# Decayed attention in two-level stages: products of 192 columns, a buffer of further decayed queries, and a seventh level of 64x64

## The reference, cut to what matters

```
S_t = diag(g_t) S_{t-1} + k_t v_t^T        o_t = S_t^T q_t
decay[i, j] = exp(sum of log g over j+1..i)     for j <= i
scores[i, j] = sum over d of  q[i, d] * k[j, d] * decay[i, j, d]
o[i] = sum over j <= i of scores[i, j] v[j]
```

## Time and profile before

| what | value |
|---|---|
| median of 3 runs | 1010.59 us (1009.25 to 1010.59) |
| the profiled execution's own time | 1010.97 us |
| its span, first to last instruction | 1009.1 us |
| PE busy | 989.7 us, 98% of the span |
| POOL busy | 752.5 us, 75% |
| DVE busy | 549.5 us, 54% |
| ACT busy | 486.5 us, 48% |
| mean granted TensorE clock | 0.990 |

### The profile page before, as it was taken

The page is one execution under the profiler, slowest core; times in us unless marked ns, Lnnn a source line. Parts: engine busy times, 40 slices in busy tenths (PEclk is TensorE's granted clock), DMA queues, the critical chain, the costliest instruction groups (busy, mean ns, idle before and its releaser), DMA issues.

```text
span 1009.1 us, 21532 instructions
## 1 busy us (share of the span) xinstructions
PE 989.7 (98%) x8151; PEld 973.7 (96%) x8151; DVE 549.5 (54%) x931; ACT 486.5 (48%) x749; POOL 752.5 (75%) x588
## 2 busy tenths in 40 slices
PE   9999999999999999999999999999999999999996
PEld 7999999999999999999999899999999989999996
DVE  5945984547644444601874783476656574445103
ACT  6634324446654444444566643433264564444541
POOL 2896666666999888999389844667549539999993
PEclk9999999999999999999999998999999999999998
DMA  9564434343565555565454223443226736665661
GB/s 308 178 200 142 125 106 134 120 143 97 177 194 182 177 169 174 159 176 183 135 172 147 88 85 101 126 136 116 86 82 189 236 101 198 194 190 181 185 179 56
DMA packets 48345, 154.63 MB, mean 153 GB/s; under 512 B 6060, under 2 KB 11188, under 8 KB 48280
## 3 DMA queue, kind: packets, MB, share of 16 engines
q1 hardware_dynamic: 46128, 151.33, 48.6%
q10 hardware_dynamic: 2152, 2.38, 0.7%
HBM read 151.59 MB, written 2.10 MB: 152 GB/s over the span
## 4 chain that ended last, share of the span: by engine, by line
PE 87%; DVE 6%; ACT 3%; POOL 2%; DMA 1%; issue 1%; SPq 0%; DVEq 0%; ACTq 0%
PE panel L1721 70%; PE panel L1779 3%; PE aux L1880 3%; POOL wlo L644 1%; DMA memk<-in_mem_panels 1%; PE aux L2134 1%; PE aux L2145 1%; PE panel L1815 1%; PE aux L2107 1%; DVE h L1107 1%; DVE tmp L1101 1%; PE aux L2175 1%; PE aux L2184 1%; PE aux L1787 1%; DVE xl L1090 1%
## 5 line engine op out<-in xcount | busy, mean ns | idle before, releaser
L644 POOL TENSOR_TENSOR wlo<-raw,whi 128x512 fp32r<-128x512 f32 x548 | 727.7, 1357 | 234.7 <-ACT whi L739 211.6
L1721 PE MATMUL panel<-xh,whi 128*128 128x256 f32 (+2 forms) x1440 | 416.9, 290 | 3.5 <-DVE xl L1090 1.3
L1721 PE MATMUL panel<-xh,wlo 128*128 128x256 f32 (+2 forms) x1440 | 409.9, 285 | 0.0
L1721 PE MATMUL panel<-xl,whi 128*128 128x256 f32 (+2 forms) x1440 | 409.5, 284 | 0.0
L739 ACT ACTIVATE whi<-raw 128x1024 fp32r<-128x1024 f32 x280 | 293.9, 1053 | 200.6 <-PE panel L1721 167.4
L1721 PEld LDWEIGHTS panel<-xh,whi 128*128 128x128 f32 x1440 | 273.3, 190 | 5.6 <-issue 2.0
L1721 PEld LDWEIGHTS panel<-xh,wlo 128*128 128x128 f32 x1440 | 273.3, 190 | 0.0
L1721 PEld LDWEIGHTS panel<-xl,whi 128*128 128x128 f32 x1440 | 272.8, 189 | 0.1
L1721 PE MATMUL panel<-hh,wlo 128*128 128x272 f32 (+1 forms) x352 | 100.5, 286 | 0.0
L1721 PE MATMUL panel<-hh,whi 128*128 128x272 f32 (+1 forms) x352 | 100.2, 285 | 0.0
L1721 PE MATMUL panel<-hl,whi 128*128 128x272 f32 (+1 forms) x352 | 99.9, 284 | 0.0
(11 more groups left out here) (336 smaller groups left out, 1575.2 us busy)
## 6 DMA issues: line engine op xcount, KB each, us to landing
raw<-in_panels SPq DMA_DIRECT2D x232, 512.0 KB, 3.5
raw<-in_down SPq DMA_DIRECT2D x32, 448.0 KB, 3.3
raw<-in_down SPq DMA_DIRECT2D x16, 512.0 KB, 3.5
memk<-in_mem_panels SPq DMA_DIRECT2D x4, 512.0 KB, 7.9
memx<-in_mem SPq DMA_DIRECT2D x4, 256.0 KB, 5.5
h<-in_x SPq DMA_DIRECT2D x1, 1024.0 KB, 8.6
spill<-h ACTq DMA_DIRECT2D x1, 1024.0 KB, 4.6
h<-spill ACTq DMA_DIRECT2D x1, 1024.0 KB, 7.2
```

The costliest lines, as they stand in the source:

```text
L644: ins = nc.gpsimd.tensor_tensor(wlo[:, slot, half], raw[:, slot, half], whi[:, slot, half].bitcast(f32), ALU.subtract)
L1721: ins = M(bank[:, 0:w], wt[:, slot, P * t:P * t + P], x[:, kk, c0:c0 + w], start=first and m == 0 and n == 0, stop=last and m == len(pairs ...
```

## The change

The nine levels become six stages. `STAGES` gives for each the number of banks of a group's step and the number of outputs that follow it. Stage 0 is level 0. Stages 1, 2 and 3 (blocks of b = 1, 4, 16) each do two levels at once: within four blocks of b positions the block pairs 0-1, 1-2, 2-3 (near) and 0-2, 0-3, 1-3 (far) are all made from one state of q and k, with a second buffer `far` that holds the queries of blocks 2 and 3 decayed further back. A product now has 192 columns: the queries of blocks 1 to 3, near and far. Stage 4 is the seventh level and multiplies only the 64 keys by the 64 queries that are used. Stage 5 is level 8. DVE copies each head's bank in three masked copies (192, 128 and 64 elements a partition) and multiplies quarter by quarter.

```diff
+STAGES = [(2, 1), (4, 2), (4, 2), (4, 2), (1, 1), (1, 1)]
+LAST_HALF, LAST_BLOCK = 4, 5
+PAIRED = 3 * P // 2
...
-    for n in range(18):
-        steps += [("level", n // 2, n % 2), ("out", XQ + n)]
+    n = XQ
+    for stage, (_, beside) in enumerate(STAGES):
+        for g in range(2):
+            steps += [("level", stage, g)] + [("out", n + x) for x in range(beside)]
+            n += beside
...
-        masks = at("masks", late, [P, 8, P], i32)
+        masks = at("masks", late, [P, P + 3 * PAIRED], i32)
...
+        q_and_far = at("q_and_far", ar, [P, 8, 3072])
+        q, far = (q_and_far[:, x, 0:HEADS * ROWS].rearrange("p (h r) -> p h r", h=HEADS) for x in (0, 7))
...
+            def far_queries(stage, heads):
+                b = BLOCK[stage]
+                now, qv, fv = quarters_of(TOTALS[stage], heads), parts_of(q, heads, b), parts_of(far, heads, b)
+                TT(fv[1], qv[2], bc(now[1], 3, b), ALU.mult)
+                order(TT(fv[2], qv[3], bc(now[2], 3, b), ALU.mult))
+                return TT(fv[3], fv[2], bc(now[1], 3, b), ALU.mult)
...
+                        dve.wait_ge(a_ready, 1)
+                        order(TT(q[:, heads, :], q[:, heads, :], f[:, heads, :], ALU.mult))
+                        far_queries(1, heads).then_inc(level_up[g], 1)
+                    elif stage < LAST_HALF:
...
+                                if part == 0:
+                                    aux_wait(dve, n)
+                                    made[x] = order.mark(nc.vector.copy_predicated(to[:, :, :, b:], bc(near_mask, 1, 2), got[:, :, 0]))
+                                    continue
+                                order.after(made[x])
+                                if part == 1:
+                                    made[x] = order.mark(nc.vector.copy_predicated(
+                                        to[:, :, :, 2 * b:], bc(far_mask[:, :, 0:2 * b], 1, 2), got[:, :, 1, :, 0:2 * b]))
+                                else:
+                                    nc.vector.copy_predicated(to[:, :, :, 3 * b:], bc(far_mask[:, :, 2 * b:], 1, 2),
+                                                              got[:, :, 1, :, 2 * b:]).then_inc(aux_free[n % 4], 1)
...
+                        dve.wait_ge(level_up[g], stage)
+                        a_ = order.mark(TT(two, now[2], now[3], ALU.mult))
+                        times(kv[2], now[3], b)
+                        times(qv[1], now[0], b)
+                        TT(qv[2], fv[1], bc(now[0], 3, b), ALU.mult)
+                        TT(qv[3], fv[3], bc(now[0], 3, b), ALU.mult)
+                        order.after(a_)
+                        a_ = order.mark(TT(three, now[1], two, ALU.mult))
+                        times(kv[1], two, b)
+                        order.after(a_)
+                        TT(TOTALS[stage + 1][:, heads, :], now[0], three, ALU.mult)
+                        ins = times(kv[0], three, b)
+                        if stage + 1 < LAST_HALF:
+                            order(ins)
+                            ins = far_queries(stage + 1, heads)
+                        ins.then_inc(level_up[g], 1)
...
+                        elif stage < LAST_HALF:
+                            hd, b = 4 * g + x, BLOCK[stage]
+                            for m in range(2):
+                                at_q = ROWS * hd + P * m
+                                near_and_far = q_and_far[:, 0:8:7, at_q:at_q + P].rearrange("p v (m i) -> p v m i", i=4 * b)
+                                ins = M(bank[:, PAIRED * m:PAIRED * m + PAIRED], k[:, hd, P * m:P * m + P], near_and_far[:, :, :, b:],
+                                        start=True, stop=True)
+                        elif stage == LAST_HALF:
+                            for m in range(8):
+                                hd, at_k = 4 * g + m // 2, P * (m % 2)
+                                ins = M(bank[0:64, 64 * m:64 * m + 64], k[:, hd, at_k:at_k + 64], q[:, hd, at_k + 64:at_k + P],
+                                        start=True, stop=True)
```

More of the change, by code:

```diff
@@ L144, in aux_uses @@
         elif kind == "level":
-            uses += [step + (x,) for x in range(2 if rest[0] < 8 else 1)]
+            uses += [step + (x,) for x in range(STAGES[rest[0]][0])]
         elif kind in ("scores", "probs"):
@@ L1225, in _, with quarters_of, parts_of, times @@
             split_slim(1, wglr)
+            def quarters_of(totals, heads):
+                four = totals[:, heads, :].rearrange("p h (m four) -> p h m four", four=4)
+                return [four[:, :, :, x] for x in range(4)]
+            def parts_of(t, heads, b):
+                four = t[:, heads, :].rearrange("p h (m four b) -> p h m four b", four=4, b=b)
+                return [four[:, :, :, x, :] for x in range(4)]
+            def times(part, factor, b):
+                return TT(part, part, bc(factor, 3, b), ALU.mult)
+            def far_queries(stage, heads):
[4 more added lines that the diff above has]
+                return TT(fv[3], fv[2], bc(now[1], 3, b), ALU.mult)
             for step in FIRST:
@@ L1268, in _ @@
                 if kind == "level":
-                    l, g = step[1], step[2]
+                    stage, g = step[1], step[2]
                     heads = slice(4 * g, 4 * g + 4)
-                    if l == 0 and g == 0:
-                        dve.wait_ge(s_zero, 1)
-                    if l < 8:
+                    if stage == 0:
+                        if g == 0:
+                            dve.wait_ge(s_zero, 1)
                         for x in range(2):
-                            bank, n = aux("level", l, g, x)
+                            bank, n = aux("level", 0, g, x)
                             aux_wait(dve, n)
@@ L2237, in constants @@
     j, i = np.arange(P)[:, None], np.arange(P)[None, :]
[L2238 to L2242 removed]
+    masks = [j == i]
+    for b in (1, 4, 16):
+        blocks, at_row = np.arange(P // (4 * b))[:, None, None], np.arange(P)[:, None, None, None]
+        for keys in ((0, 1, 2), (0, 1, 0)):
+            start = blocks * 4 * b + np.array(keys)[:, None] * b + np.zeros(b, int)
+            masks.append(((at_row >= start) & (at_row < start + b)).reshape(P, -1))
+    masks = np.concatenate(masks, 1).astype(np.int32)
     ang = 2 * np.pi * np.outer(np.arange(64), np.arange(WAVES)) / 64
```

82 lines of the change are left out of this document (45 added, 37 removed).

## The result

| what | before | after |
|---|---|---|
| median | 1010.59 us (1009.25 to 1010.75) | 1020.05 us (1019.51 to 1020.60) |
| ratio, 95% interval (the two medians alone give 1.009) | | 1.011 (1.0087 to 1.0134) |
| span of the profiled execution | 1009.1 us | 1018.8 us |
| mean granted TensorE clock | 0.990 | 0.984 |
| first scores step of PE starts at | 173.13 us | 182.82 us |

The change makes the kernel slower by 9.5 us; I had forecast +4.7 and a range that ended at 1019.5. The direction was right, the size was not. Executions of one and the same kernel, the kernel before too, fall into two groups some 5 to 6 us apart: in the profiles, the stretch behind the stages takes 836.0 us where the clock falls near 577 and near 600 us, 831.6 where it falls at the first place only, and 830.0 or 830.1 where it doesn't fall.

A forecast was written before the change was run, and what follows sets the result against it. PE was taken to bound the levels, with DVE close behind at 89% busy. The terms -7.0 + 3.7 + 5.5 + 2.5 gave +4.7 us, forecasting a median of 1015.3 us, range 1007.5 to 1019.5.

The forecast's parts named there:

- What PE saves: PE's products over the six stages: 30.3 us before, 23.4 after, so 7.0 us less to do.
- the 0.17: Sign for stage 1: PE passes starting more than 0.17 us apart would show the price of its reads wrong.
- First part: Ahead of group 0's stage 1 step: PE waits for three DVE multiplications taking turns with POOL halves, +3.7 us.
- Second part: DVE over the six double steps needs 55.2 us against PE's 53.9; with a 4.2 us lag, PE waits +5.5 us.
- Multiplications of 256 [...] at 0.34 are 18.3: DVE in stages 1 to 3: 54 multiplications of 256 elements at 0.34 us each, 18.3 us.
- A head costs 0.70: DVE's masked copies of 192, 128 and 64 elements: 0.70 us a head, 2.8 a step, 16.8 for six steps.
- my 14: Over the six double steps, 14 of 24 POOL halves stop DVE, costing 16.4 us.
- mostly at stage 4: Place of PE's 5.5 us of waiting for DVE: the lag is carried through earlier stages and falls due there.
- Third part: PE's clock drops to 1.2 GHz behind two waits: 0.8 us for the first fall, 1.7 for the second, +2.5.
- POOL's halves fall beside the masked copies: Rival over the double steps: at most 9 of 24 halves stop DVE, clock stays up; -5.7 us, 1004.9; chance 0.17.
- DVE is worse off: Rival: 18 halves stop DVE, or short-run copies or PE's reads cost more, or long slow clock; +10.9, 1021.5; chance 0.13.

The follow-up runs named there:

- a2: Changed kernel with stage 1's multiplications and masked copies on adjacent elements, not every fourth: first scores step at 174.79 us, against 182.82.
- a4: Changed kernel with products of ones put into PE's three waits, in banks ACT had long emptied: first scores step at 179.93 us, against 182.82.
- e1_products_alone: Changed kernel with only stage 1's multiplications on adjacent elements, masked copies keeping their short runs: first scores step at 176.76 us, against 182.82.

## Why the prediction was wrong

- *What PE saves, -7.0*: right. Its own terms give 6.9, the measured steps 7.2. The passes of 192 columns start 0.1625 apart (2.60 / 16), under the 0.17 that I had set as the bound, so PE's new reads in runs of three cost nothing. Missed: an output behind products of 64 columns takes 3.03 and not 2.84, +0.4 in all.
- *First part, +3.7*: right in mechanism and nearly in size; 4.15. The turns were as worked out (3.57 in a2, without the distance), and what was missing is the distance of four elements, 0.6.
- *Second part, +5.5*: **this is the step that failed.** Its words "Multiplications of 256 [...] at 0.34 are 18.3" and "A head costs 0.70" price all stages by rows of neighbouring elements. In stage 1 nine of the twelve cost 0.53 and a head's copies 0.81 (0.59 in stage 2, less than I had said). And the sum ran over six steps as if they were alike. DVE's total was no more than I had said: its six steps took about 52 us (27.5 in stage 1, 13.3 in stage 2, 11 in stage 3), not 55.2, which by my own sum would have left PE a wait of 2 us. What made the waits is that 27.5 of them fell in stage 1's two steps, where my prices and a third of my halves come to about 21, against PE's 16.5. PE, whose next step needs the banks that DVE's copies release, can be no more than two outputs ahead; what it waits there isn't given back by stages 2 and 3, where DVE needs 5.5 to 7.1 us a step against PE's 8.3. The halves that stopped DVE between 104 and 152 us were nine, fewer than my 14, yet eight of them in stage 1. With the clock held up (a4), all of DVE's waits are worth 179.93 - 173.13 + 6.6 = 13.4 us, where the two parts together said 9.2. That, and 0.4 each for the outputs and the clock, is the whole miss of 5.0.
- *"mostly at stage 4"*: wrong. That wait is 1.4 us, and shows only in runs in which PE comes to stage 4 earlier.
- *Third part, the clock, +2.5*: 2.9. The argument that the first fall is mostly hidden by DVE held (0.3 us, where I had 0.8). The nearness of the sums is luck: I took each fall to last 3.4 us and it lasted 6.8, so the second cost 3.0 and not 1.7, and that it isn't more in the end comes of a wait at stage 4 that I didn't have in this part.
- *The rivals*: the first, "POOL's halves fall beside the masked copies", had as its condition that no more than 9 of the 24 halves stop DVE. That came true, and the kernel was slower all the same, because what counts is the stage in which they fall. "DVE is worse off", with "copies of short runs or PE's new reads cost more than their neighbours", came nearest at 1021.5. Its first clause was the truth; its 18 halves and its price of the reads weren't. I gave it 0.13, having looked for a row that priced the new copies and found none; I should have looked for one that priced a distance of four elements, and bounded both by its absence.

## What to carry over

Price an operation by a row with the same distance between elements, not only the same size: a change that fuses two levels turns a distance of two floats into one of four, and DVE's cost rises by a factor of 1.6 (0.55 us against 0.34). When two engines hand small buffers back and forth, make the sum for each stage, since what is lost in the slow one isn't won back in the fast one. A fusion can be taken where it is cheap and left out where it isn't.

## What was not expected of the hardware

- DVE: 0.34 us for 256 elements at distances of one and two floats, 0.47 to 0.55 as soon as one operand is at four, 0.63 at eight.
- In two runs a half of POOL stood behind nine DVE multiplications, for 5.3 us in one of them, while elsewhere the two take turns after each instruction.
- How long the granted clock stays at 0.50 behind a wait varies: 6.83 us behind waits of 3.52, 4.20, 4.47 and 4.92, 10.24 behind one of 6.29, but behind 4.15 it was 6.83 in one run and 3.41 in another, and behind 3.57 likewise. Behind a wait of 1.65 (e1_products_alone) it didn't fall.
